# Two-layer encoder in split fp32r: last stream tile moved behind the last turns, attention rows scaled in two lots, six low parts a layer made by GpSimd

## The reference, cut to what matters

```python
u = x @ w_in
y_att = rms_norm(windowed_gqa(aq, ak, av, sink), att_g)      # 8 heads of 64, window of 128
y_ml = mlstm_group(u[mq, mk], u[mv], u[mo], u[gates], ...)   # conv + silu, mLSTM, sigmoid(u[mo])
return concatenate([y_att, y_ml]) @ w_out
```

## Time and profile before

| | |
|---|---|
| median of 3 runs | 2218.72 us (2217.67 to 2223.54) |
| the profiled execution | 2220.75 us |
| its span, first to last instruction | 2219.1 us |
| PE busy | 2100.4 us, 95% of the span |
| DVE, ACT, POOL busy | 1316.9, 978.8, 230.5 us |
| mean granted clock of PE | 0.977 of full speed |

### The profile page before, as it was taken

How to read it: one execution, slowest core, us unless ns; L and a number is a source line. 1 busy time by engine, 2 the same in 40 slices (tenths; PEclk the granted TensorE clock), 3 DMA queues, 4 the chain that set the end, 5 groups by cost and what they waited for, 6 DMA issues and landing times.

```text
span 2219.1 us, 30120 instructions
## 1 busy us (share of the span) xinstructions
PE 2100.4 (95%) x10816; PEld 1670.5 (75%) x10816; DVE 1316.9 (59%) x2001; ACT 978.8 (44%) x1568; POOL 230.5 (10%) x268
## 2 busy tenths in 40 slices
PE   7989989999999899999898999999999989999997
PEld 6877767888878577777677886788888767777774
DVE  3875487822454765666877637782235476665557
ACT  3554565232422455555245557533333135555553
POOL 0000032000000321001100002300000032100004
PEclk9999999999998999999899999999999889999999
DMA  4154212321102699999511112033110059999995
GB/s 154 58 195 133 78 56 97 114 76 57 57 29 98 251 369 373 387 378 356 188 58 39 39 39 95 22 132 114 68 66 20 32 227 383 376 371 377 376 378 220
DMA packets 78526, 384.78 MB, mean 173 GB/s; under 512 B 10472, under 2 KB 11864, under 8 KB 43608
## 3 DMA queue, kind: packets, MB, share of 16 engines
q1 hardware_dynamic: 55264, 327.31, 38.9%
q0 software_dynamic: 10096, 30.38, 3.8%
q10 hardware_dynamic: 13064, 25.75, 3.1%
HBM read 352.27 MB, written 46.07 MB: 180 GB/s over the span
## 4 chain that ended last, share of the span: by engine, by line
PE 74%; DVE 14%; ACT 7%; issue 2%; DMA 1%; POOL 0%; DVEq 0%; ACTq 0%; POOLq 0%; SPq 0%
PE bank L2216 30%; PE bank L2736 10%; PE bank L2710 8%; PE bank L2700 8%; PE bank L2437 5%; DVE weight_slots_parts L1453 2%; PE bank L2547 2%; PE bank L2468 2%; PE bank L2237 1%; PE bank L2676 1%; ACT scratch L1075 1%; PE bank L2591 1%; PE bank L2607 1%; DVE scratch L1614 1%; ACT weight_slots_parts L973 1%
## 5 line engine op out<-in xcount | busy, mean ns | idle before, releaser
L1922 DVE TENSOR_TENSOR weight_slots_parts<-weight_slots,mixer_region_parts 128x2048 fp32r<-128x2048 f32 x140 | 321.6, 2317 | 85.1 <-ACT mixer_region_parts L1277 84.9
L2216 PE MATMUL bank<-weight_slots_parts,x_transposed_parts 128*128 128x512 f32 x864 | 281.4, 408 | 2.8 <-DVE weight_slots_parts L1453 2.8
L2216 PE MATMUL bank<-x_transposed_parts,weight_slots_parts 128*128 128x512 f32 (+1 forms) x1024 | 264.0, 345 | 7.2 <-DVE mixer_region L1566 4.0
L1277 ACT ACTIVATE mixer_region_parts<-weight_slots 128x2048 fp32r<-128x2048 f32 x140 | 260.9, 1908 | 22.1 <-ACT x_transposed L1352 18.1
L1453 DVE TENSOR_TENSOR weight_slots_parts<-weight_slots,weight_slots_parts 128x2048 fp32r<-128x2048 f32 x58 | 132.9, 2292 | 193.5 <-ACT weight_slots_parts L973 192.7
L2736 PE MATMUL bank<-weight_slots,x_transposed 128*128 128x512 f32 x560 | 247.6, 595 | 0.0
L2710 PE MATMUL bank<-mixer_region_parts,x_transposed_parts 128*128 128x256 f32 x1120 | 207.4, 283 | 0.2 <-DVE weight_slots_parts L1922 0.2
L2216 PEld LDWEIGHTS bank<-x_transposed_parts,weight_slots_parts 128*128 128x128 f32 x1024 | 180.6, 193 | 29.8 <-DVE mixer_region L1566 5.3
L2700 PE MATMUL bank<-mixer_region_parts,x_transposed_parts 128*128 128x512 f32 x560 | 192.1, 414 | 5.1 <-ACTq L1317 2.3
L2736 PEld LDWEIGHTS bank<-weight_slots,x_transposed 128*128 128x128 f32 x560 | 104.0, 191 | 118.6 <-issue 103.0
L2216 PEld LDWEIGHTS bank<-weight_slots_parts,x_transposed_parts 128*128 128x128 f32 x864 | 163.6, 195 | 36.6 <-DVE weight_slots_parts L1453 4.5
(11 more groups left out here) (319 smaller groups left out, 3524.2 us busy)
## 6 DMA issues: line engine op xcount, KB each, us to landing
weight_slots<-in_w_gate SPq DMA_DIRECT2D x70, 1024.0 KB, 7.2
weight_slots<-in_w_up SPq DMA_DIRECT2D x70, 1024.0 KB, 7.0
weight_slots<-in_w_down SPq DMA_DIRECT2D x70, 1024.0 KB, 7.5
weight_slots<-in_w_in SPq DMA_DIRECT2D x20, 1024.0 KB, 5.0
slots_y<-x_transposed ACTq DMA_DIRECT2D x66, 256.0 KB, 7.2
weight_slots<-in_wkv_mem SPq DMA_DIRECT2D x16, 1024.0 KB, 4.8
slots_y<-in_consts SPq DMA_DIRECT2D x6, 2304.0 KB, 17.7
weight_slots<-in_w_out SPq DMA_DIRECT2D x8, 1024.0 KB, 5.2
```

Of the source, the lines that this page charges most:

```text
L1277: nc.scalar.activation(hi, raw, ACT.Copy).then_inc(moe.high_ready, 1)
L1922: v.tensor_tensor(lo, raw, hi.bitcast(F32), ALU.subtract).then_inc(moe.low_ready, 1)
L2216: ins = pe.matmul(ps, lhs[i](k), rhs[j](k), start=k == 0 and a == 0, stop=k == KD - 1 and a == 2)
```

## The change

- `PER_SLOT` gives slot 11 three stream tiles and slot 12 one: ("o",5,1) is computed in slot 12, behind `turn_probs` of group 11 and in front of its `pv`. PE spreads the maxima for the first mLSTM group in front of this tile.
- ACT takes the `rstd` of the attention rows in two lots: chunks 0 to 2 in slot 9, chunks 3 and 4 in slot 11. DVE scales chunks 0 to 2 at the end of slot 10 and chunks 3 and 4 in slot 12.
- wo0 is split behind ("o",2,1) in slot 10 rather than behind ("o",3,1) in slot 11.
- The low parts of mq0, mq1, mv0, mv1, mo0 and mo1 are made by POOL, each as four TENSOR_TENSOR instructions of 128x512, as soon as the high part is there. DVE no longer makes them.
- ACT handles the last tile of slot 11, ("o",4,1), in slot 12, behind the drains of the turned probabilities.

```diff
-PER_SLOT = [3, 3, 2, 3, 3, 2, 4, 4, 4, 4, 4, 4]
-STARTS = [sum(PER_SLOT[:i]) for i in range(13)]
+PER_SLOT = [3, 3, 2, 3, 3, 2, 4, 4, 4, 4, 4, 3, 1]
+STARTS = [sum(PER_SLOT[:i]) for i in range(14)]
...
 SPLIT_BEHIND[("v", 2, 1)] = SPLIT_BEHIND.pop(("v", 3, 1))
+SPLIT_BEHIND[("o", 2, 1)] = SPLIT_BEHIND.pop(("o", 3, 1))
...
+POOL_LOW = ("mq0", "mq1", "mv0", "mv1", "mo0", "mo1")
...
                     nc.gpsimd.memset(va[:, :, :, MD:MD + 1], 1.0).then_inc(ones_made, 1)
+                    for name in POOL_LOW:
+                        pool.wait_ge(w_hi, len(SPLITS) * l + SPLITS[name] + 1)
+                        pool.wait_ge(w_lo, len(SPLITS) * l + SPLITS[name])
+                        lo, raw, hi = half_lo(name, 4), half_raw(name, 4), half_hi(name, 4).bitcast(F32)
+                        for k in range(4):
+                            ins = nc.gpsimd.tensor_tensor(lo[:, k, :], raw[:, k, :], hi[:, k, :], ALU.subtract)
+                        ins.then_inc(w_lo, 1)
...
-                        if i == 11:
-                            rstd(st[:, 20:25], st[:, 20:25], 5, 1.0 / ATT, eps_rms).then_inc(att_rs, 1)
+                        if i in (9, 11):
+                            lo, hi = (20, 23) if i == 9 else (23, 25)
+                            rstd(st[:, lo:hi], st[:, lo:hi], hi - lo, 1.0 / ATT, eps_rms).then_inc(att_rs, 1)
                             own(att_rs)
 
-                        for t in ended + w[:-1] if i < 12 else ():
+                        for t in ended + w[:-1]:
...
+                            dve.wait_ge(w_lo, len(SPLITS) * now[0] + SPLITS[name])
                             v.tensor_tensor(half_lo(name), half_raw(name), half_hi(name).bitcast(F32), ALU.subtract).then_inc(w_lo, 1)
-                        own(w_lo)
+                        dve.wait_ge(w_lo, len(SPLITS) * now[0] + SPLITS[name] + 1)
...
-                            if STREAM[i - 1] in SPLIT_BEHIND:
+                            if STREAM[i - 1] in SPLIT_BEHIND and SPLIT_BEHIND[STREAM[i - 1]] not in POOL_LOW:
                                 low_weights(SPLIT_BEHIND[STREAM[i - 1]])
...
                         if i == 12:
-                            dve.wait_ge(att_rs, 2 * l + 1)
-                            for c in range(NC - 1):
+                            dve.wait_ge(att_rs, 3 * l + 2)
+                            for c in (3, 4):
                                 attention_scaled(c)
...
+                        if i == 10:
+                            dve.wait_ge(att_rs, 3 * l + 1)
+                            for c in range(3):
+                                attention_scaled(c)
...
-                                    dve.wait_ge(att_rs, 2 * l + 2)
+                                    dve.wait_ge(att_rs, 3 * l + 3)
                                     attention_scaled(NC - 1)
...
+                        if i == 12:
+                            unit_ready("running_max")
+                            spread_maxima(0)
                         if w and i:
                             stream_tile(w[0])
                         if i:
-                            if i == 12:
-                                unit_ready("running_max")
-                                spread_maxima(0)
                             c, jp = GROUP_ORDER[i - 1]
```

More of the change, by code:

```diff
@@ L204, in slot_tiles @@
 def slot_tiles(i):
-    return STREAM[STARTS[i]:STARTS[i + 1]] if 0 <= i < 12 else []
+    return STREAM[STARTS[i]:STARTS[i + 1]] if 0 <= i < 13 else []
 def score_tiles(i):
@@ L437, in slot_of, with half_raw @@
             return (now[0] * len(UNITS) + UNIT[name]) % SLOTS
-        def half_raw(name):
+        def half_raw(name, k=KD):
             s = slot_of(name) * 4096
-            return by_k(ring[:, s + 2048:s + 4096])
+            return by_k(ring[:, s + 2048:s + 4096], k)
         def half_hi(name, k=KD):
```

## The result

The changed kernel took 2238.85 us (median of 7 runs, 2235.88 to 2242.33), the kernel before beside it 2223.54 us (7 runs). The ratio is 1.0079, 95% interval 1.0062 to 1.0096: slower by 15.3 us in the medians, 17.5 by the ratio. The prediction had 2235.5 us, a loss of 16.8, and gave slower 0.81. The profiled execution took 2241.26 us, its span 2239.2, mean granted clock 0.974.

The account below looks back on a forecast made before the run. The prediction took PE as the bound, busy 2100.4 of 2219.1 us, other engines costing only PE's waits and clock. Its terms, 11.2 + 6.2 + 0 - 0.6 = +16.8 us on the median 2218.72, gave 2235.5 us, range 2222 to 2242.

Parts of the forecast that it names:

- Part 1: PE's four waits for mv1 and mo1, two a layer: each low part 2.8 us later from POOL, +11.2 us.
- Part 2: PE's clock behind the four waits for mv1 and mo1: falls each time, 1.55 us each, +6.2 us.
- one stretch of 3.30 us: PE after 80.60 to 84.30: granted clock 0.53, near the 1.2 GHz level, costing 1.55 us.
- Rival 1: Behind PE's late low parts the clock stays at 2.4 GHz: +8.6 us, 2227 us; chance 0.22.
- Part 3: DVE without its six low parts: 2.29 us saved each, but no gain, POOL holding DVE up at mq0 and mv0: 0.
- The +2.4 us: DVE at mq0 and mv0, both layers: by the skill page's exclusion rule, a loss of 4 x 0.6 us.
- Rival 3: DVE was the bound of slots 2 to 6, its relief 9.4 us a layer: -7.7 us, 2211 us; chance 0.07.
- Rival 2: POOL hardly holds DVE, slot 3 begins 2.3 us earlier; relief of 9.2 cancels lateness of 11.2: 2220.5 us; chance 0.12.
- Part 4: End of the slots, moved tile, scalings and wo0 split: gain of only 0.3 us a layer, -0.6 us.
- the wait of 1.42 us: PE's wait for turned probabilities at the end of the slots: should go, moving to a later wait.
- the one of 2.18: PE's later wait, 2.18 us, for a low part of the turned rows at the slots' end: should grow.

Follow-up runs that it names:

- experiment 2: The change, but POOL writes zeros for mq0, uses one-operand pieces for mv0, and ACT's small slot 9 instructions follow mo1's high part: 2228.85 us, ratio 1.0041.
- POOL's part alone: The kernel before with the six low parts made by POOL and nothing else of the change: 2234.75 us, ratio 1.0063.
- experiment 3: First tiles with mv1 and mo1 sum their high-part products first: on the change 2224.55 us, ratio 1.0028; on the kernel before 2213.61 us, ratio 0.997.
- the moves alone: The change with its moved tile, scalings and wo0 split, but all six low parts made by DVE: 2219.4 us, ratio 0.9998.
- Experiment 5: Kernel before, plus high-part-first sums and later mq0, mv0 low parts on DVE: 0.9981; those plus wo0, tile, scaling moves mended: 0.9946; mended moves only: 0.9959.
- all three edits: Kernel before with high-part-first sums, mq0 and mv0 low parts later on DVE, and mended moves of tile, scalings and wo0 split: 2205.29 us, ratio 0.9946.

## Why the prediction was right, point by point

**Part 1, mv1 and mo1 by POOL: right, its closeness by luck.** Predicted 4 x 2.8 = 11.2 us; the waits grew by 11.3, to 3.15 to 3.92 us where I had 3.3 to 3.8. POOL's four pieces took 4.96 and 4.94 us where I had 5.1, nearer to my rows than to the 4497 ns of the Trainium skill, page "GPSIMD Engine Reference", section "Performance versus the Vector engine". But one step was missed: the new `rstd` of slot 9 stands on ACT between the square of a chunk and mo1's high part. I costed the split of `rstd` at nothing without naming what was queued behind it on ACT. ACT's timeline after the change:

```profile
240.01 0.30 ACT L939 ACTIVATE small<-small,constants 128x3 f32<-128x3 f32 x1
240.34 0.20 ACT L940 ACTIVATE small<-small 128x3 f32<-128x3 f32 x1
240.58 1.92 ACT L984 ACTIVATE weight_slots_parts<-weight_slots 128x2048 fp32r<-128x2048 f32 x1
```

It costs 0.55 us a layer (3.92 against 3.37 in experiment 2), 1.1 in all. POOL's lateness by itself was 10.2 us, as the kernel with POOL's part alone shows (waits of 13.0 us where before had 2.8): I had it 1.0 too large, and the missed step covered that.

**Part 2, the clock: right in kind, small in size.** I took a fall behind all four waits, 1.55 us each, from one stretch of 3.30 us. It fell behind all four, for 1.7, 1.7, 2.9 and 2.8 us: 9.1 instead of 6.2. This was the largest miss of the sum; I had named a longer fall as possible and left it out of the middle value. Rival 1 (clock kept) is out, by the windows of the change and by experiment 3, where shortening the waits brought back more than their length.

**Part 3, DVE's relief: right.** Taken as 0. DVE gave back the 2.29 us in three instructions held up by POOL; the scores came 0.2 us later (115.18 against 114.98), and the four low parts in question left the time where it was (ratio 0.9997). Line 1569 (1582 after), with one SBUF input, is held too: 0.92 us for 0.29. This is what the Trainium skill's page "SBUF — State Buffer" says under "Who interferes with whom", and the trace agrees for POOL's two-operand pieces. Its rule counts every GpSimd instruction that reads SBUF, and there experiment 2 differs: beside one-operand pieces DVE's product of two SBUF tiles kept its 0.69 us. The +2.4 us that I had worked out from the rule came out as 0.04 us by the maxima of slot 6 in layer 0 (0.36 by the turns in front of them) and 0.63 in layer 1, 0.7 in all. Rival 3 (DVE the bound of slots 2 to 6) had a true half: with POOL's reads away for mq0 and halved for mv0 the turns of slot 6 came at 178.82 in place of 182.62, 3.8 us where it needed 9 a layer. Rival 2 failed by the same exclusion.

**Part 4, the end of the slots: right.** Predicted 0.3 us a layer gained, because DVE's slot 10 is overfull and the wait of 1.42 us moves into the one of 2.18. That wait is now 2.84 us, the one of 1.42 is gone, and from the scores of slot 10 to the last wait the change takes 0.2 us less than before in each layer; the moves alone measured 0.9998. In between, the scores of slot 11 came 4.8 us later, measured from those of slot 10, as forecast. Experiment 5 shows the cause by mending it.

**The sum.** 16.8 predicted, 15.3 (medians) to 17.5 (ratio) measured. With the waits at 11.3, the clock at 9.1, part 3 at 0.7 and the end at -0.4 the sum would have been 20.7, which the slots of the one profiled execution bear out (20.2). The medians show less, but the interval of the ratio (1.0062 to 1.0096, or 13.8 to 21.3 us) holds both sums. So the mechanism is shown term by term, while that 16.8 lies so near the measured 17.5 is in part luck.

The best version found is that with all three edits and no low part on POOL: 0.54% below the kernel before, 1.3% below the change.

## What to carry to other kernels

Before you give work to an idle engine, look who stands behind it: the same work cost some 4 us at two places of a layer and nothing that could be measured at four others. Where a consumer does stand behind a slow producer, first change the order of its own work, so that what needs the late operand comes last; here that took back most of the loss and also improved the kernel before. And read a split of small instructions by its queue: what stands behind them on their engine pays for them, even if they are off every chain themselves.

## What the runs showed of the hardware

- DVE instructions with both ends in SBUF were held beside POOL's two-operand pieces (an addition of 4 columns 1.13 us in place of 0.16), much less beside one-operand pieces (0.45; a product of two SBUF tiles kept its 0.69). DVE instructions that read PSUM beside the same pieces kept their time: lines 1576, 1577 and 1579 took 0.54, 0.48 and 0.48 us, as in the row of convolutions before.

```profile
109.54 0.54 DVE L1576 TENSOR_SCALAR mixer_region<-bank,conv_taps 128x256 f32<-128x256 f32 x1
110.12 0.48 DVE L1577 SCALAR_TENSOR_TENSOR mixer_region<-bank,conv_taps,mixer_region 128x255 f32<-128x255 f32 x1
```

- PE's granted clock fell behind each of the change's waits of 3.15 to 3.92 us for a low part, behind none of 0.51 to 1.36 us for one that I looked at, and behind one of two of 2.14 us at the same place of the two layers (0.65 and 1.00). Added up until the clock was back, one fall cost 1.7 to 2.9 us. One place that no edit touched (slot 3 to slot 4 of layer 1) differed by 1.1 us from one profiled execution to another, by the clock behind the waits of slot 3.
- A piece of 128x512 numbers on POOL took 1.26 to 1.74 us: 4.94 to 4.99 for four when DVE was idle (mv1, mo0, mo1), 5.66 beside DVE's work (mq0).
